# Forgetting attention on one core: the sign of the scores turned round, the negation of the row maximum dropped, and the softmax scaling moved from VectorE to ScalarE

## What is computed

```python
def forgetting_attention(q, k, v, log_f):
    scale = Dh ** -0.5
    c = jnp.cumsum(log_f, axis=1).transpose(0, 2, 1)
    for qb in range(S // Q_BLOCK):              # 8 blocks of 128 queries
        lo = qb * Q_BLOCK
        hi = lo + Q_BLOCK
        s = jnp.einsum('bqhd,bkhd->bhqk', q[:, lo:hi], k[:, :hi]) * scale
        s = s + c[:, :, lo:hi, None] - c[:, :, None, :hi]
        s = jnp.where(causal, s, -jnp.inf)
        p = jax.nn.softmax(s, axis=-1)
        outs.append(jnp.einsum('bhqk,bkhd->bqhd', p.astype(v.dtype), v[:, :hi]))
```

## Time and profile before

| | us |
|---|---|
| median of 3 runs | 1906.48 (1903.08 to 1912.17) |
| the profiled execution | 1907.9, its span 1906.3 |
| stretch of the attention stage | 825 to 1018, 193 |
| PE, DVE, ACT busy in that stretch | 160.7, 140.2, 101.1 |
| PE, DVE, ACT busy in the whole span | 1727.3, 1060.8, 848.5 |

### The profile page before, as it was taken

The page is one execution under the profiler, slowest core; times in us unless marked ns, Lnnn a source line. Parts: engine busy times, 40 slices in busy tenths (PEclk is TensorE's granted clock), DMA queues, the critical chain, the costliest instruction groups (busy, mean ns, idle before and its releaser), DMA issues. The chain is left out here.

```text
span 1906.3 us, 22922 instructions
## 1 busy us (share of the span) xinstructions
PE 1727.3 (91%) x8515; PEld 1375.1 (72%) x8515; DVE 1060.8 (56%) x1211; ACT 848.5 (45%) x861; POOL 130.7 (7%) x179
## 2 busy tenths in 40 slices
PE   4999999999999998988887989949999999999980
PEld 3788888888986887867776879836677777777750
DVE  4343434341214003257774342658988888888856
ACT  5233334241212212135553030227777877777751
POOL 2200000000000000011110000010000000000005
PEclk9999999999999999999998989969999999999995
DMA  5722213223331333534434250189999999999937
GB/s 175 206 89 84 103 66 113 74 88 129 137 111 45 100 118 110 191 133 177 177 121 154 102 167 21 58 302 395 391 398 393 394 400 393 394 400 396 399 123 275
DMA packets 147070, 386.02 MB, mean 203 GB/s; under 512 B 11448, under 2 KB 70920, under 8 KB 142928
## 3 DMA queue, kind: packets, MB, share of 16 engines
q1 hardware_dynamic: 133760, 338.97, 47.8%
q0 software_dynamic: 8384, 29.63, 5.2%
q10 hardware_dynamic: 4880, 16.82, 2.2%
HBM read 317.96 MB, written 67.42 MB: 202 GB/s over the span
## 5 line engine op out<-in xcount | busy, mean ns | idle before, releaser
L1510 DVE TENSOR_TENSOR e_l<-e_raw,e_h 128x2048 fp32r<-128x2048 f32 x192 | 439.4, 2291 | 67.2 <-ACT e_h L1504 67.0
L1504 ACT ACTIVATE e_h<-e_raw 128x2048 fp32r<-128x2048 f32 x192 | 367.8, 1916 | 85.1 <-PE ps L1539 50.2
L196 PE MATMUL ps<-uh,w_h 128*128 128x512 f32 x1024 | 319.8, 394 | 20.7 <-DVE ul L838 13.1
L196 PE MATMUL ps<-ul,w_h 128*128 128x512 f32 x1024 | 318.3, 392 | 0.0
L196 PE MATMUL ps<-uh,w_l 128*128 128x512 f32 x1024 | 318.2, 392 | 0.0
L180 DVE TENSOR_TENSOR w_l<-w_raw,w_h 128x2048 fp32r<-128x2048 f32 x38 | 87.1, 2291 | 350.8 <-ACT w_h L176 350.8
L196 PEld LDWEIGHTS ps<-uh,w_h 128*128 128x128 f32 x1024 | 194.3, 190 | 62.3 <-issue 22.1
L196 PEld LDWEIGHTS ps<-ul,w_h 128*128 128x128 f32 x1024 | 194.2, 190 | 40.8
L196 PEld LDWEIGHTS ps<-uh,w_l 128*128 128x128 f32 x1024 | 194.0, 189 | 40.5
L1526 PE MATMUL ps<-e_h,e_xth 128*96 128x512 f32 x512 | 205.2, 401 | 5.8 <-DVE e_l L1510 2.7
L1526 PE MATMUL ps<-e_h,e_xtl 128*96 128x512 f32 x512 | 202.9, 396 | 0.0
(11 more groups left out here) (254 smaller groups left out, 2250.6 us busy)
## 6 DMA issues: line engine op xcount, KB each, us to landing
e_raw<-w_exp_gate SPq DMA_DIRECT2D x64, 1024.0 KB, 11.9
e_raw<-w_exp_up SPq DMA_DIRECT2D x64, 1024.0 KB, 12.3
e_raw<-w_exp_down SPq DMA_DIRECT2D x64, 1024.0 KB, 12.8
w_raw<-w_in SPq DMA_DIRECT2D x28, 1024.0 KB, 5.5
qk_d<-qk SPq DMA_DIRECT2D x16, 1024.0 KB, 4.2
at_qk<-qk_d SPq DMA_DIRECT2D x8, 2048.0 KB, 8.9
y_d<-e_y ACTq DMA_DIRECT2D x32, 384.0 KB, 6.4
y_d<-zeros POOLq DMA_DIRECT2D x22, 384.0 KB, 11.1
```

Of the source, the lines that this page charges most:

```text
L196: mm = pe.matmul(ps[:, h * HALF:(h + 1) * HALF], w[:, k, :], u[:, k, h * HALF:(h + 1) * HALF], start=first, stop=last)
L1504: act.activation(self.e_h[m % SPLIT][:, :, :], self.e_raw[slot][:, :, :], ACT.Copy).then_inc(self.e_hi[m % SPLIT], 1)
L1510: dve.tensor_tensor(self.e_l[slot][:, :, :], self.e_raw[slot][:, :, :], self.e_h[m % SPLIT][:, :, :].bitcast(F32), ALU.subtract).then_inc( ...
```

## The change

The queries are stored with the opposite sign and the bias without its negation, so that what L1077 leaves in SBUF is the score with the opposite sign. It takes the row minimum in place of the maximum; ScalarE's exp multiplies its input by -1 and takes that minimum directly as its bias, so L1081 is gone. The fill of the mask and the start value of the reduction change sign. VectorE keeps the reciprocal; the multiplication of the row (L1089) becomes a Copy activation of ScalarE with the reciprocal as scale, issued in the step after the tile's own exp, behind that step's exp (new line 1042).

```diff
-        SCALE = (1.0, HD ** -0.5)
+        SCALE = (1.0, -HD ** -0.5)
...
-                act.activation(bias[:, :], c_sum[:, :], ACT.Copy, scale=-1.0).then_inc(bias_out, 1)
+                act.activation(bias[:, :], c_sum[:, :], ACT.Copy).then_inc(bias_out, 1)
...
                 def exponent(i, n):
                     keys = (block_of(n) + 1) * P
-                    act.wait_ge(negated, tiles * i + n + 1)
-                    act.activation(sb[n % SB][:, 0:keys], sb[n % SB][:, 0:keys], ACT.Exp,
-                                   bias=small[:, n % 2, 1:2], accum_out=small[:, n % 2, 2:3]).then_inc(exped, 1)
+                    act.wait_ge(least, tiles * i + n + 1)
+                    act.activation(sb[n % SB][:, 0:keys], sb[n % SB][:, 0:keys], ACT.Exp, scale=-1.0,
+                                   bias=small[:, n % 2, 0:1], accum_out=small[:, n % 2, 1:2]).then_inc(exped, 1)
+
+                def scale(i, n):
+                    keys = (block_of(n) + 1) * P
+                    act.wait_ge(inverted, tiles * i + n + 1)
+                    act.activation(sb[n % SB][:, 0:keys], sb[n % SB][:, 0:keys], ACT.Copy,
+                                   scale=small[:, n % 2, 2:3]).then_inc(scaled, 1)
...
                     if n < tiles:
                         exponent(i, n)
+                    if tile := back(i, n, 1):
+                        scale(*tile)
...
                         dve.tensor_tensor_reduce(out=sb[n % SB][:, 0:keys], in0=k_.ps[n % 2][:, 0:keys],
-                                                 in1=bias[c][:, 0:keys], scale=1.0, scalar=NEG, op0=ALU.add,
-                                                 op1=ALU.max, accum_out=small[:, n % 2, 0:1]).then_inc(maxed, 1)
-                        dve.wait_ge(maxed, tiles * i + n + 1)
-                        dve.tensor_scalar(small[:, n % 2, 1:2], small[:, n % 2, 0:1], -1.0, None, ALU.mult)\
-                            .then_inc(negated, 1)
+                                                 in1=bias[c][:, 0:keys], scale=1.0, scalar=-NEG, op0=ALU.add,
+                                                 op1=ALU.min, accum_out=small[:, n % 2, 0:1]).then_inc(least, 1)
                     if tile := back(i, n, 1):
                         i_, m = tile
-                        b, keys = m % 2, (block_of(m) + 1) * P
+                        b = m % 2
                         dve.wait_ge(exped, tiles * i_ + m + 1)
-                        dve.reciprocal(small[:, b, 3:4], small[:, b, 2:3]).then_inc(inverted, 1)
-                        dve.wait_ge(inverted, tiles * i_ + m + 1)
-                        dve.tensor_scalar(sb[m % SB][:, 0:keys], sb[m % SB][:, 0:keys], small[:, b, 3:4], None,
-                                          ALU.mult).then_inc(scaled, 1)
+                        dve.reciprocal(small[:, b, 2:3], small[:, b, 1:2]).then_inc(inverted, 1)
```

More of the change, by code:

```diff
@@ L893, in attention @@
         qk_in, v_in, bias_in, stored = k_.qk_in, k_.v_in, k_.bias_in, k_.o_stored
-        names = ("mask", "masked", "s_mm", "maxed", "negated", "exped", "inverted", "scaled", "t_mm", "hi", "lo", "pv_mm", "o_out")
-        masks, masked, s_mm, maxed, negated, exped, inverted, scaled, t_mm, hi, lo, pv_mm, o_out = (sem("at_" + n) for n in names)
+        names = ("mask", "masked", "s_mm", "least", "exped", "inverted", "scaled", "t_mm", "hi", "lo", "pv_mm", "o_out")
+        masks, masked, s_mm, least, exped, inverted, scaled, t_mm, hi, lo, pv_mm, o_out = (sem("at_" + n) for n in names)
         turns, tiles = NH // 2, 2 * NT
@@ L932, in load_qk @@
                 def load_qk(i, c):
-                    sp.wait_ge(maxed, tiles * i - tiles + NT * (c + 1))
+                    sp.wait_ge(least, tiles * i - tiles + NT * (c + 1))
                     k_.load_head_qk(sp, i, c)
@@ L957, in _ @@
                 pool.wait_ge(masks, 1)
-                pool.affine_select(out=mask[:, :], in_=mask[:, :], compare_op=ALU.is_ge, fill=NEG, base=0,
+                pool.affine_select(out=mask[:, :], in_=mask[:, :], compare_op=ALU.is_ge, fill=-NEG, base=0,
                                    pattern=[[-1, P]], channel_multiplier=1).then_inc(masks, 1)
@@ L967, in diagonal @@
                     else:
-                        pool.wait_ge(maxed, tiles * i + n)
+                        pool.wait_ge(least, tiles * i + n)
                     pool.tensor_tensor(block, block, mask[:, :], ALU.add).then_inc(masked, 1)
@@ L980, in scores @@
                         pe.wait_ge(qk_in[c], 16 * (i + 1))
-                    later(pe, maxed, tiles * i + n - 1)
+                    later(pe, least, tiles * i + n - 1)
                     queries = slice(qb * P, (qb + 1) * P)
```

## The result

The changed kernel takes 1950.55 us (median of 4 runs, 1948.9 to 1952.13) against 1909.33 for the kernel before beside it (4 runs); the ratio is 1.0222, with a 95% interval of 1.0197 to 1.0247. That is +41 us, where +37 was forecast against the 1906.48 known then.

What follows compares the result with a forecast made beforehand. PE led the busy time and waited for DVE in the wide tiles. With the copies on ACT a head takes 16.9 + 5.0 + 5.0 = 26.9 us against 22.3, +37 over eight heads: 1943.5 us, range 1926 to 1963.

Steps and rivals of the forecast that it cites:

- What bounds the kernel: Attention stage: PE leads, waiting for DVE in wide tiles; PE's 27.7 us of waits are the most to give back.
- DVE's 45 us: DVE in the stage loses 64 scalings, 35.4 us, and 64 negations, 9.8 us; removing the negation alone was taken as 0.
- The copy's duration: ACT's 64 new scaled copies last as long as exps of the same widths, 773 ns in the mean.
- The two rules: Skill pages on ACT copies: a cycle table making the sum about 6 us lower, and advice to multiply on VectorE.
- The sum for one head: ACT at full clock: own work 16.9, long wait 5.0, new waits 5.0, together 26.9 us against 22.3, +4.6 per head.
- I take the cost as unchanged: Granted clock in the stage: a half-speed stretch keeps costing 1.5 us; up to +18 us left in the range.
- short waits: New waits of ACT for PE's transposes between a tile's scaling and its high part: 0.92 us whole, 5.0 us per head.
- small point: PE before transposes: waits for DVE's low parts mostly gone, its waits now put down to ACT's line 1042.
- Rival 2: PE's transposes run beside other ACT work, covering the new waits: head 21.9 us, 1903, no change; chance 0.06.
- rival 3: DVE's relief in the wide tiles counts more than ACT's load: PE's 27.7 us of waits vanish, 1879 us; chance 0.04.
- Rivals 4 and 5: Clock low for most of the stage, 1967 to 2006, chance 0.09; function table reloaded between Exp and Copy, +164, chance 0.01.

Runs made afterwards that it cites:

- sign only: The change without its scaling on ScalarE (minimum for maximum, no negation, scaling stays on VectorE), against the kernel before: 1907.53 us, ratio 0.9997.
- plain copy: The changed kernel with ScalarE's copy left without its scale per row: whole time 2285.32 us (other experts picked), stage shorter by 6.2 us, copy 675 ns.
- later transposes: Transposes, high parts, low parts and value products one step later: 1891.73 us with scaling on VectorE and the sign part, 1900.08 us on the changed kernel.
- narrow kernel: The changed kernel with ScalarE's scaling doing only the first 128 columns of each row: whole time 2212.87 us (other experts picked), stage shorter by 26.1 us.
- exchanged pair: The changed kernel with ScalarE's scaling of the tile before put ahead of the tile's exp, not behind it: 1915.8 us, ratio 1.0043 to the kernel before.

## Why the prediction was right, step by step

- **What bounds the kernel.** Right: PE's waits for VectorE were what the change could give back, and none of it came, since ACT and PE together now set a longer time per tile than VectorE did.
- **DVE's 45 us.** Its busy time in the stage fell from 138.6 to 97.9 us (95 forecast), and it is waited for almost nowhere. The sum took the sign part at 0; sign only gave 0.9997.
- **The copy's duration.** 767 ns against 773.
- **The two rules.** The cycle table of the Trainium skill ("VectorE: DVE Perf Modes", the section on the TRN2 errata) gives, as an estimate by that page, (224 + 576) / 1.2 = 667 ns for the mean width of 576 columns. The plain copy measured 675, which agrees; the one with a scale per row measured 767, which does not. By the page's figure the sum would be 6 us lower; the measured 767 is on the side of the rows. Its advice to multiply on VectorE ("ScalarE: Activation LUTs", rules for kernel authors) was borne out here, 1891.7 against 1900.1 us with the later transposes (two chips; heads of 21.0 to 21.3 against 22.1 to 22.3 us), though the order of instructions was worth more.
- **The sum for one head.** Forecast at full clock 26.9. The two heads shown, 27.4 and 29.2 us, are both with low stretches. The forecast counted ACT's overlap with the wait; as the profile counts, it was 17.7 busy (16.9 and seven times 0.11) and 9.2 idle. The head of 27.4 us has 17.7 busy and 9.7 idle. The single waits of that head: 0.75, 0.74, 0.75 for tiles 8, 7, 6 (0.81 forecast) and 0.26 after tile 5 (0.33 forecast), so a little under; for tiles 4 and 3 over, 1.21 and 1.12 where 0.81 and 0.69 were forecast, with the clock at 0.50 from 874 to 876:

```profile
874.13 0.60 ACT L1030 ACTIVATE at_pth<-ps 128x512 fp32r<-128x512 f32 x1 [1.21 <-PE ps L996]
876.84 0.49 ACT L1030 ACTIVATE at_pth<-ps 128x384 fp32r<-128x384 f32 x1 [1.12 <-PE ps L996]
```

With these two at 0.74 and 0.72, as in a head of the narrow kernel at clock 1.00, it would take 26.6 us, an estimate: no head of the changed kernel ran wholly at full clock.

- **The step that was mis-sized** is the clock: "I take the cost as unchanged". Seven heads of the changed kernel take 28.4 us in the mean (827.55 to 1026.52), 1.5 above the 26.9; seven of the kernel before take 23.3 (829.09 to 991.91), 1.0 above 22.3. The difference, 0.5 us in each of eight heads, is the 4 us between +37 and +41. Measured from the estimate of 26.6, the clock costs the changed kernel 1.8 us per head where I took 1.0, and the short waits give 0.3 of that back. The reason that I gave for taking no extra cost, that part of it falls where PE waits for ACT, does not hold for tiles 4 and 3: ACT waits for the transposes of tile 4 themselves, and PE's scores stand ahead of those of tile 3. The same kernel measured again came out at +48, with a clock of 0.86: the range held that too, the +37 was 11 us off.
- **The small point** that PE's waits for low parts would mostly go: on its matmuls none is left. The profile puts 30.7 us in 18 waits of the weight loads down to VectorE's low parts, but in the head at 883.3 the last low part was done earlier. For tile 5 it ended at 897.37, the scaling at 898.00, and the load began at 898.12; tile 4 shows the same (900.34, 900.79, 900.91), so what these loads waited for was the scaling.

```profile
896.35 1.02 DVE L1075 TENSOR_TENSOR at_ptl<-ps,at_pth 128x512 fp32r<-128x512 f32 x2 [1.59 <-ACT at_pth L1030]
```

```profile
898.12 0.53 PEld L996 LDWEIGHTS ps<-ident,at_s 128*128 128x128 f32 x5 [2.08 <-DVE at_ptl L1075]
```

- **The rivals.** Rival 2 (new waits covered) is what the exchanged pair nearly makes true, +7 us; rival 3 (faster) needs an order in which no wait stands between scaling and high part, and with that it did come, 0.9957, though by the clock: heads of 22.1 to 22.3 us are those of the kernel before at full clock. Rivals 4 and 5 did not occur: the clock is 0.89, and there is one table load.

## What to carry to other kernels

Before moving an operation to the engine with the most idle time, look at what stands right behind it in that engine's order: if the next instruction needs, through another engine, the result of the one just added, a wait comes in every turn; here the move cost 41 us, and with the same work one place earlier in that order 7. An instruction is priced by its place, so try the order first: one step more between producer and consumer gave 0.992 with no other change. And where gaps bring the granted clock down, they cost more than themselves: in the kernel before, a head with a low stretch takes 1.5 us more than one without. So compare stretches of like clock before crediting a few microseconds to an edit.

## What the runs showed of the hardware

- Extra matmuls on PE in its gaps made the kernel faster: 235.9 us of stage with a granted clock of 0.86, 227.9 with 0.96, although PE did 128 matmuls of 512 columns more. In the changed kernel the clock fell to half (1.2 of 2.4 GHz) at about 900 us, behind a stretch in which PE stood still before its transposes for 2.0, 1.9 and 1.7 us; in the kernel before it fell at 890.0 behind two waits of 0.9 us.
- The kernel before repeats a head in 22.2 or 22.3 us at a granted clock of 1.00 and in 23.7 to 23.9 at 0.93.
- A scale per row read from SBUF adds 92 ns to a ScalarE copy from SBUF (767 against 675 ns), as it adds 90 ns to one from PSUM.
